# Two norm scales laid out as rows through a scratch in DRAM instead of over TensorE, and VectorE's weight scaling moved ahead of an attention output split

## The reference, cut to what matters

```python
def rmsnorm(x, g):
    xf = x.astype(jnp.float32)
    y = xf * lax.rsqrt(jnp.mean(xf * xf, axis=-1, keepdims=True) + EPS) * g.astype(jnp.float32)
    return y.astype(x.dtype)
...
proj = h @ w_in                      # h = rmsnorm(x, g), first layer
q, k, v, gate, glr = jnp.split(proj, [...], axis=-1)
gk = jax.nn.log_sigmoid((glr @ w_gk2 + b_gk).astype(f32)) / GLA_GATE_NORM
...
z = h @ w_in[i]                      # the same in the second block
qa, ka, va, qb, kb, vb, ga, gb = jnp.split(z, split_at, axis=-1)
```

## Time and profile before

| | us |
|---|---|
| median of 3 runs | 975.13 |
| lowest, highest | 973.6, 975.2 |
| the profiled execution | 973.7 |
| its span, first to last instruction | 972.0 |
| TensorE busy in the span | 963.4 |
| VectorE, ScalarE, GpSimd busy | 660.8, 492.3, 60.0 |

### The profile page before, as it was taken

How to read it: one execution, slowest core, us unless ns; L and a number is a source line. 1 busy time by engine, 2 the same in 40 slices (tenths; PEclk the granted TensorE clock), 3 DMA queues, 4 the chain that set the end, 5 groups by cost and what they waited for, 6 DMA issues and landing times.

```text
span 972.0 us, 13088 instructions
## 1 busy us (share of the span) xinstructions
PE 963.4 (99%) x5368; PEld 827.1 (85%) x5368; DVE 660.8 (68%) x938; ACT 492.3 (51%) x589; POOL 60.0 (6%) x128
## 2 busy tenths in 40 slices
PE   9999999999999999999999999999999999999997
PEld 8888888888889878888888889988888888888886
DVE  5877786555669967656666658767766766566665
ACT  5555454444447855544444453555564544444454
POOL 3451000000001001000000013000000000000000
PEclk9999999999999999999999999999999999999999
DMA  8663767676563235766765555543266465555551
GB/s 264 200 196 133 229 183 223 209 208 206 173 216 119 99 93 192 217 206 207 203 218 204 189 176 174 164 162 121 76 229 210 156 216 173 195 195 179 191 193 54
DMA packets 114707, 176.31 MB, mean 181 GB/s; under 512 B 5260, under 2 KB 77656, under 8 KB 114648
## 3 DMA queue, kind: packets, MB, share of 16 engines
q1 hardware_dynamic: 114472, 175.28, 55.9%
q10 hardware_dynamic: 176, 0.20, 0.1%
HBM read 173.76 MB, written 1.70 MB: 181 GB/s over the span
## 4 chain that ended last, share of the span: by engine, by line
PE 95%; DVE 3%; DMA 1%; issue 0%; ACT 0%; SPq 0%; POOL 0%; ACTq 0%; DVEq 0%
PE ps L367 92%; PE ps L371 3%; DVE wlo L1235 1%; DMA raw<-in_a_w_in 1%; DVE M L1243 0%; DVE cc L1721 0%; DVE RR L1243 0%; DVE M L1235 0%; SPq L2940 0%; DVE M L1239 0%; DVE cc L1720 0%; ACT RR L2153 0%; ACT xs L2150 0%; DVE cc L1235 0%; DVE x L1243 0%
## 5 line engine op out<-in xcount | busy, mean ns | idle before, releaser
L367 PE MATMUL ps<-whi,RR 128*128 128x512 f32 (+1 forms) x1556 | 397.2, 387 | 0.0
L1235 DVE TENSOR_TENSOR wlo<-raw,whi 128x1024 fp32r<-128x1024 f32 (+1 forms) x323 | 373.1, 1197 | 21.0 <-ACT whi L2153 20.6
L2153 ACT ACTIVATE whi<-raw 128x2048 fp32r<-128x2048 f32 (+1 forms) x161 | 301.1, 1873 | 162.7 <-PE ps L367 137.7
L367 PEld LDWEIGHTS ps<-whi,RR 128*128 128x128 f32 x1556 | 284.0, 188 | 55.6 <-issue 0.9
L367 PE MATMUL ps<-RR,whi 128*128 128x512 f32 (+1 forms) x1264 | 261.2, 351 | 0.1
L367 PEld LDWEIGHTS ps<-RR,whi 128*128 128x128 f32 x1264 | 200.6, 190 | 27.1 <-issue 1.5
L367 PE MATMUL ps<-wlo,RR 128*128 128x512 f32 (+1 forms) x778 | 220.5, 385 | 0.0
L367 PEld LDWEIGHTS ps<-wlo,RR 128*128 128x128 f32 x778 | 144.3, 188 | 29.3 <-DVE wlo L1235 0.2
L1235 DVE TENSOR_TENSOR M<-M,ps 128x512 f32<-128x512 f32 (+1 forms) x57 | 38.7, 682 | 171.7 <-ACT M L2153 167.4
L367 PEld LDWEIGHTS ps<-RR,wlo 128*128 128x128 f32 x1016 | 138.4, 191 | 9.1 <-DVE wlo L1235 0.7
L367 PE MATMUL ps<-RR,wlo 128*128 128x256 f32 x1016 | 144.6, 283 | 0.0
(11 more groups left out here) (109 smaller groups left out, 420.8 us busy)
## 6 DMA issues: line engine op xcount, KB each, us to landing
raw<-in_w_up SPq DMA_DIRECT2D x32, 1024.0 KB, 6.3
raw<-in_w_down SPq DMA_DIRECT2D x32, 1024.0 KB, 5.7
raw<-in_w_ff SPq DMA_DIRECT2D x32, 1024.0 KB, 5.2
raw<-in_w_in SPq DMA_DIRECT2D x23, 1024.0 KB, 5.1
raw<-in_a_w_in SPq DMA_DIRECT2D x10, 1024.0 KB, 5.4
raw<-in_a_w_out SPq DMA_DIRECT2D x4, 1024.0 KB, 5.3
raw<-in_b_w_q SPq DMA_DIRECT2D x4, 1024.0 KB, 5.5
raw<-in_b_w_out SPq DMA_DIRECT2D x4, 1024.0 KB, 5.1
```

The source lines that it names most:

```text
L367: return pe.matmul(out, lhsT, rhs, start=start, stop=stop, skip_group_check=True)
L1235: return dve.tensor_tensor(out, a, b, op)
L2153: return act.activation(out, in_, ACT.Copy, **k)
```

## The change

Three things. First, for s = 0 and s = 4 `diagonals` and both `rows_scale` are gone; SP writes the two columns `st[:, 4:6]` to a scratch in DRAM (`scale_row_out`, 256 elements of 4 bytes) when GpSimd has made them, and later reads them back as a row to all 128 partitions, twice (`scale_row`, 128 x 2 rows of 1 KB, 256 KB in all), when the write has landed. `rb(s)` then waits for that load. s = 2 stays as it was. `par` reads from the scratch and is issued earlier. Second, in `window()` at i = 3 alone `lows(0)` goes behind `shares(2)`. Third, in `attentions()` `fu_shares` goes ahead of `fu_lows` in the four steps that have both (`fu_lows` 1 to 4).

```diff
--- before.py
+++ after.py
@@ -727,7 +727,6 @@
         K.value["w_used", j] = K.full(("glr", 0))
 
     low_rank()
-    rows_scale(0)
     tile = ("g", 1)
     b = take(tile, 2)
     for w in due(K.dma("g16", 6)):
@@ -993,7 +992,6 @@
     norm_rest(4)
     next(products_a)
     run_all((products_a, 1))
-    rows_scale(4)
 
 
 
@@ -1368,7 +1366,7 @@
         dve.tensor_copy(RB[:, 256:512], b[:, 0:256]).then_inc(*K.emptied(("rbt", s)))
 
     def rb(s):
-        return [K.empty(("rbt", s)), K.at("p8", s)]
+        return [K.dma("rb%d" % s, 1) if s in (0, 4) else K.empty(("rbt", s)), K.at("p8", s)]
 
     def turn_parts(name, half, free):
         for i in range(2):
@@ -1504,11 +1502,8 @@
     ev = {}
 
     def ev_qk(f):
-        if f == 0:
-            diagonals(0)
         if f == 256:
             early()
-            rows_scale(0)
         for f2 in {0: [], 256: [0, 256]}.get(f, [f]):
             tile = ("qk", f2)
             for w in due(K.full(tile), *rb(0)):
@@ -1754,10 +1749,12 @@
                 shares(0)
             if i < 8:
                 soft(i)
-            if 3 <= i:
+            if 3 < i:
                 lows(i - 3)
             if 1 < i < 9:
                 shares(i - 1)
+            if i == 3:
+                lows(0)
             yield
 
     def halves(n):
@@ -1801,8 +1798,6 @@
     t.then_inc(*K.up("x_lnf"))
     squares("4b", K.at("x_lnf"))
     run_all((products_a, 1))
-    diagonals(4)
-    rows_scale(4)
 
     def ev_k(f):
         tile = ("kb", f)
@@ -1999,8 +1994,8 @@
         fu_shares(2)
         fu_max(3)
         yield
+        fu_shares(3)
         fu_lows(1)
-        fu_shares(3)
         fu_turned(2)
         fu_max(4)
         yield
@@ -2009,13 +2004,13 @@
         fu_max(5)
         yield
         for h in range(2, 4):
+            fu_shares(h + 3)
             fu_lows(h)
-            fu_shares(h + 3)
             fu_turned(h + 2)
             fu_max(h + 4)
             yield
+        fu_shares(7)
         fu_lows(4)
-        fu_shares(7)
         fu_turned(6)
         yield
         fu_lows(5)
@@ -2950,6 +2945,18 @@
             dst = V.raw_block(K, j).rearrange("p (k n) -> p k n", k=kt)
             sp.dma_start(dst, src.rearrange("(k p) n -> p k n", p=128)).then_inc(*K.up_dma("w%s" % at, j))
 
+    def scale_row_out(s):
+        for w in due(K.at("rstd", s)):
+            sp.wait_ge(*w)
+        sp.dma_start(bass.AP(tensor=A["scr4"].tensor, offset=s * T, ap=[[1, 128], [128, 2]]), V.st[:, 4:6],
+                     allow_slow_non_contiguous=True).then_inc(*K.up_dma("rb%d" % s, 0))
+
+    def scale_row(s):
+
+        load("rb%d" % s, 1, V.RB[:, 0:2 * T].rearrange("p (a t) -> p a t", a=2),
+             bass.AP(tensor=A["scr4"].tensor, offset=s * T, ap=[[0, 128], [0, 2], [1, T]]), K.dma("rb%d" % s, 0),
+             *([K.empty(("kk",))] if s else []))
+
     def rows(a):
         return a.rearrange("a (k p) -> (a k) p", p=128) if len(a.shape) == 2 else a.rearrange("(k p) -> k p", p=128)
 
@@ -2981,8 +2988,10 @@
     load("tab", 0, S["tab"][0:32, 0:16], A["rel_table"])
     load("tab", 1, S["tab"][0:32, 16:28], A["rel_bias_2"])
     load("sel", 0, S["sel"], A["c_sel"])
+    scale_row_out(0)
     load("msk", 0, S["mask"][:, :], A["c_mask"])
     weights_to(7)
+    scale_row(0)
     for i, (dst, name) in enumerate((("onorm", "a_onorm"), ("qg", "q_norm_g_2"), ("kg", "k_norm_g_2"),
                                      ("sink", "b_sinks"))):
         load("bc", i, S[dst], spread(A[name]))
@@ -3023,8 +3032,11 @@
                 tensor=A["scr3"].tensor, offset=127 - 16 * a + 4 * 272 * g, ap=[[8 * 272, 16], [272, 4], [1, 128]]))
     load("lnf", 0, M[:, 0:1024], spread(A["ln_final"]))
 
-    weights_to(103)
-    load("par", 0, V.st[:, 8:10], V.RB[0:1, 0:T].rearrange("a (p two) -> a p two", two=2), K.empty(("rbt", 4)))
+    weights_to(97)
+    scale_row_out(4)
+    weights_to(99)
+    scale_row(4)
+    load("par", 0, V.st[:, 8:10], bass.AP(tensor=A["scr4"].tensor, offset=4 * T, ap=[[2, 128], [1, 2]]))
     weights_to(109)
     load("bg", 0, V.BG, spread(A["b_gate_2"][:, 0:1024]), K.at("rope", 1))
     weights_to(113)
@@ -3052,6 +3064,7 @@
         A["scr1"] = nc.dram_tensor("scr1", (16, 16, 400), F32, kind="Internal").ap()
         A["scr2"] = nc.dram_tensor("scr2", (16, 4, 544), F32, kind="Internal").ap()
         A["scr3"] = nc.dram_tensor("scr3", (16, 8, 272), F32, kind="Internal").ap()
+        A["scr4"] = nc.dram_tensor("scr4", (5, T), F32, kind="Internal").ap()
         S = {
             "raw": sb("raw", [128, 3, SLOT]), "hi": sb("whi", [128, NS, SLOT], F32R),
             "lo": sb("wlo", [128, NS, SLOT], F32R),
```

## The result

| | before | changed |
|---|---|---|
| median, us | 975.16 (973.60 to 975.41, 4 runs) | 988.03 (987.34 to 988.93, 4 runs) |
| profiled execution, us | 973.7 | 987.3 |
| its span, us | 972.0 | 985.6 |

The account below looks back on a forecast made before the run. TensorE was taken to bound the kernel, busy 963.4 of 972.0 us. First norm +4.5, s = 4 -0.24, window -0.34 and full attention -0.17 gave +3.8 us: 978.9 us on the median of 975.13, range 977.2 to 981.0.

Parts of the forecast that it names:

- The write's price: First norm: the scratch write lands 2.4 us after issue, at about 22.2, at most 5.8 us, at 25.5.
- 31.0: First norm: time in us when the gate products start, against 26.49 before, 4.5 us later (3.7 to 5.4).
- The load: First norm: the row's load, queued behind 2 MB of blocks 5 and 6, lands at 29.1 (28.3 to 30.0).
- Rival 1: TensorE's clock falls in the new 4.7 us gap, 1.6 us lost: +5.4, 980.5 us; chance 0.23.
- 3.3 us: Behind the first norm's gap: time at the low clock, yielding half the work, 1.6 us lost.
- Rival 2: First norm: row's load is not last in the queue, lands 2.4 us after issue; -0.45, 974.7 us; chance 0.10.
- Rival 3: Behind the first norm, the gated attention's chain stalls TensorE again by up to 0.9 us: +4.7, 979.8; chance 0.10.
- s = 4: Norm at s = 4: TensorE saves the scale's matmul, without a wait: -0.24 us.
- 8 us of cover: Norm at s = 4: the row's load lands at 578.4 at the latest, its first use is at 586.51.
- Window: Exchange in the window: weights ready earlier with lows(0) behind them, shortening TensorE's 0.35 us wait: -0.34 us.
- Full attention: Exchanges in the full attention: only head 7's weights make TensorE wait, other three save nothing: -0.17 us.

Follow-up runs that it names:

- Experiment 2: Kernel before plus both exchanges, the s = 4 norm through DRAM, and the first norm's write to the scratch, which nobody reads: 978.01 us, ratio 1.0039.
- two by two: Four runs of the changed kernel with a two-line write; row's load behind or ahead of blocks 5 and 6, common or own 1 KB: 979.95, 979.36, 978.25, 973.37 us.
- ahead, common: Changed kernel with the write as two lines and the row's load ahead of the mask and blocks 5 and 6, same 1 KB for all partitions: 978.25 us.
- behind, own: Changed kernel with the write as two lines and the row's load behind blocks 5 and 6, reading each partition's own 1 KB stretches of x: 979.36 us.
- experiment 11: Changed kernel with 80, then 64 matmuls on constants in TensorE's gap ahead of the gate products, results unused: 989.89 and 987.02 us.
- ahead, own: Changed kernel with two-line write and the row's load ahead of the mask and blocks 5 and 6, each partition reading own 1 KB stretches of x: 973.37 us.

## Why the prediction was wrong, and where it was right

**The write's price, the step that failed.** The prediction bounded it by 2.4 and 5.8 us, from the mask and a row to 128 partitions, and wrote that even the upper bound lies before the transfer could run. Both rows are loads of long runs, 512 bytes and 1 KB; the write is 256 elements of 4 bytes next to each other. It took 8.67 us, the load behind it was issued at 28.28 instead of 22.5, and that is 5.8 of the 8.1 us by which the gate products missed 31.0. The upper end was no bound, since neither row shared the form. It was not free either: SP issues the load only when the write has landed, so a landing at 25.5 would have held the issue 3 us past 22.5. The Trainium skill has warnings that fit: DMA: Bandwidth & Descriptors, Specifications, says that below 512 bytes a DMA does read-modify-write, and the section Rules for kernel authors says that a strided last dimension becomes one descriptor for each element. The runs agree in part: 128 elements landed in 4.13 us, two lines in 1.7 to 2.6 us; but 256 elements 512 bytes apart landed within 2.3 us, so size and count alone don't make the price. Measured is that the price came with small elements, many, and side by side. That the read-modify-writes of neighbouring elements wait for each other is a reading of this, not shown.

**What the write does to others.** The prediction looked only at who waits for it. Experiment 2 shows that 1 KB nobody reads costs 5.2 us, by holding blocks 5 and 6 and, behind that, by the clock. Why a write that moves so little holds them is open.

**The load: size near, cause half right.** 6.6 us were forecast (28.3 to 30.0 as the landing) because 2 MB stood ahead. It took 8.90, the other 2.3 of the 8.1 us. The queue by itself is worth 3.6 us by the two by two; the same 1 KB read 256 times is worth as much by itself and was not in the working. With both at work, as in the change, the queue adds 1.7 us. The 5.8 us of `a_onorm` have the same form, a row read for all partitions, and the prediction put all of it down to the queue; how it divides there was not tried. The Trainium skill's fit (DMA: Bandwidth & Descriptors, Anatomy of one DMA), made for DMAs that GpSimd issues, gives an estimate of 2.6 us. The nearest that any run came is 3.18, issued by SyncE, with distinct addresses and nothing ahead.

**The clock.** Rival 1, with a chance of 0.23, came true as a mechanism, but its total of 980.5 did not, and the gap was 12.9 us, not 4.7. The shorter gap would have done: with 4.2 us (ahead, common) and 4.6 us (behind, own) the clock fell as well. Its price was 1.6 us and measured 2.34; the low clock lasted until about 44.4, over 5 us behind the gate products, and not 3.3. The six other runs with a gap of 4.2 to 11.4 us lost 1.5 to 2.9 us in the same stretch, in no order of the gap's length. The 3.3 us were read from matmuls at the start whose windows show a granted clock of 1.00, so no row showed the low level there; their pace, 0.23 us each against the 0.11 of experiment 11, is half. That a kernel which waits for DMA restarts at the low clock (the Trainium skill, TensorE: Matmul & The Clock Gate, HAM oscillation) agrees with this trace.

**Rivals 2 and 3.** Rival 2 is refuted in its form: the load lands late even without a queue. Rival 3 did not show: with the clock kept, the 60.30 us behind the gate products are unchanged.

**s = 4.** TensorE has no wait, as forecast; the gain is 0.44 us where 0.24 were forecast. The prediction read the matmul's price from the start of the next group, 0.24 us later. But the matmul stands in the trace as two (x2 in the earlier trace rows), and the stretch around it, 3.26 us before and 2.82 now, shows what both take. For the DMAs the 8 us of cover were thinner than thought. SP and ScalarE there:

```profile
578.95 0.37 SPq L2951 DMA_DIRECT2D scr<-st  x1
584.51 2.64 SPq L2946 DMA_DIRECT2D raw<-in_w_in  x2
589.11 0.86 SPq L2935 DMA_DIRECT2D RB<-scr  x1
...
594.20 1.92 ACT L2148 ACTIVATE whi<-raw 128x2048 fp32r<-128x2048 f32 x1 [7.35 <-DMA raw<-in_w_in]
```

The write lands after some 10 us, and so, with a median of 9.4 for the two and 8.90 for the first, does the load: about 599.0, against a first use at 600.65 that still waits for TensorE. 1.6 us were left of 8.

**The exchanges.** Window: -0.34 forecast, -0.33 measured, by the step as written. Full attention: -0.17 forecast, -0.50 measured. The 0.17 is there; the other 0.33, the wait behind the transposes for the split `fu_turned(6)`, was overlooked: the prediction asked only who waits for the weights, and not who waits for what VectorE does behind them.

**The miss as a sum.** Of the 9.9 us between forecast and traces (13.6 against 3.8, 3.75 before rounding), the write is 5.8, the load 2.3 and the clock 2.3, and against them stand 0.3 of the full attention and 0.2 at s = 4.

## What to carry to other kernels

These transfers had a price for their form, not for their bytes: the write of 1 KB took from 1.7 to 10 us. Before sending a column of small factors through DRAM, look at how many elements land side by side and at what else is in flight, because here the loads queued with it paid too. The way over DRAM took 17.6 us in the first norm (19.59 to 37.18) and some 20 at s = 4; the matmul that does the same costs 0.44 us of a full TensorE. So the way over DRAM pays only where there is more cover than that, as at s = 4. When a row of the trace serves as a bound, ask whether it shares the form of what is to be priced, and when it has two possible causes, carry both.

## What the runs showed of the hardware

- 256 elements of 4 bytes written side by side to DRAM: 8.0 us with nothing queued behind, 8.7 (and 10.2 at s = 4) with weight blocks behind; in the case of 8.7 us, with 2 MB behind it, the DMA engines moved 19 to 31 GB/s. 128 of 8 bytes: 4.1. 256 of 4 bytes 512 bytes apart: under 2.3. 2 of 512 bytes: 1.7 to 2.6.
- 256 reads of 1 KB with nothing ahead: 3.2 us from distinct places (196 GB/s in a window), 6.7 to 7.9 from the same 1 KB (46 to 71 GB/s in windows).
- In every run with a gap of 4.2 to 12.9 us without matmuls ahead of the gate products the granted clock fell to 0.50 (1.2 GHz). The 16 matmuls behind a gap of 4.2 us (ahead, common) took 3.62 us, behind one of 4.6 us (behind, own) 3.78. Experiment 2, with a wait of 3.6 us later on, shows 0.71 in the window around it. With a gap of 0.5 us (ahead, own) the 16 took 2.18.
- The scale's matmul at s = 4 (128x128 by 128x256, two rows in the trace) cost TensorE 0.44 us.
